# Modulation weights in 64 pieces of 32 rows by quarter columns, with the sum over partitions on VectorE instead of TensorE

## The reference

```
c_act = silu(c)
for i in range(2):
    mod = c_act @ w_ada[i] + b_ada[i]              # w_ada[i]: 1024 x 6144
    sh_a, sc_a, g_a, sh_f, sc_f, g_f = split(mod, 6)
    h = rmsnorm(x) * (1 + sc_a) + sh_a
    m = neighbourhood_attention(h) if i == 0 else mla(h)
    x = x + g_a * m
    h = rmsnorm(x) * (1 + sc_f) + sh_f
    f = swiglu(h) if i == 0 else moe(h)            # moe: 8 experts, top 2
    x = x + g_f * f
return rmsnorm(x) * final_norm
```

## Time and profile before

| | us |
|---|---|
| three runs | 1257.86, 1258.61, 1263.98 |
| median of the three | 1258.61 |
| profiled execution: span from the first to the last instruction | 1258.0 |
| mean granted TensorE clock, as a share | 0.996 |

### The profile page before, as it was taken

How to read it: one execution, slowest core, us unless ns; L and a number is a source line. 1 busy time by engine, 2 the same in 40 slices (tenths; PEclk the granted TensorE clock), 3 DMA queues, 4 the chain that set the end, 5 groups by cost and what they waited for, 6 DMA issues and landing times.

```text
span 1258.0 us, 20244 instructions
## 1 busy us (share of the span) xinstructions
PE 1224.1 (97%) x7668; PEld 1086.8 (86%) x7668; DVE 1016.2 (81%) x1095; ACT 779.0 (62%) x992; POOL 93.1 (7%) x111
## 2 busy tenths in 40 slices
PE   9989999999999999999999999999999999999995
PEld 7978999987998799998897777898989898989884
DVE  6797899996756588777756578989898989898987
ACT  5765666644655455443346556777777777777764
POOL 0020000000562100000002202000000000000020
PEclk9999999999999999999999999999999999999998
DMA  9953997679944569998973239999999999999991
GB/s 322 377 200 102 337 314 270 246 289 252 250 159 162 181 215 325 332 349 308 382 253 97 79 140 394 379 406 355 401 351 409 348 408 349 408 345 411 347 410 73
DMA packets 163981, 369.08 MB, mean 293 GB/s; under 512 B 24420, under 2 KB 96559, under 8 KB 157511
## 3 DMA queue, kind: packets, MB, share of 16 engines
q1 hardware_dynamic: 157345, 350.72, 78.0%
q10 hardware_dynamic: 5094, 12.11, 2.5%
q0 software_dynamic: 1472, 5.28, 1.1%
HBM read 360.72 MB, written 14.70 MB: 298 GB/s over the span
## 4 chain that ended last, share of the span: by engine, by line
PE 71%; DVE 12%; ACT 4%; issue 4%; DMA 3%; SPq 3%; POOL 2%; ACTq 0%; DVEq 0%
PE ps L1341 20%; PE ps L795 7%; PE ps L797 7%; PE ps L796 7%; PE ps L1368 6%; PE ps L807 4%; PE ps L809 4%; PE ps L811 4%; DVE wlo L1893 3%; SPq L712 2%; PE ps L859 2%; PE ps L867 2%; DMA raw<-in_moe_w_gu 2%; DVE third_lo L1893 2%; DVE wlo L1885 1%
## 5 line engine op out<-in xcount | busy, mean ns | idle before, releaser
L1406 ACT ACTIVATE whi<-raw 128x1024 fp32r<-128x1024 f32 x186 | 192.6, 1057 | 152.0 <-PE ps L797 96.1
L1885 DVE TENSOR_TENSOR wlo<-raw,whi 128x1024 fp32r<-128x1024 f32 x186 | 227.1, 1248 | 72.8 <-ACT whi L1406 69.3
L795 PE MATMUL ps<-ahi,whi 128*128 128x256 f32 x832 | 234.3, 282 | 0.3 <-ACT qT L1591 0.3
L796 PE MATMUL ps<-alo,whi 128*128 128x256 f32 x832 | 231.8, 279 | 0.0
L797 PE MATMUL ps<-ahi,wlo 128*128 128x256 f32 x832 | 231.8, 279 | 0.0
L1893 DVE TENSOR_TENSOR wlo<-raw,whi 128x1792 fp32r<-128x1792 f32 (+1 forms) x96 | 199.3, 2089 | 24.4 <-ACT whi L1420 24.3
L1420 ACT ACTIVATE whi<-raw 128x1792 fp32r<-128x1792 f32 (+1 forms) x96 | 167.5, 1758 | 55.9 <-PE ps L1368 24.0
L795 PEld LDWEIGHTS ps<-ahi,whi 128*128 128x128 f32 x832 | 156.9, 189 | 1.7 <-issue 0.8
L796 PEld LDWEIGHTS ps<-alo,whi 128*128 128x128 f32 x832 | 156.7, 188 | 0.7 <-issue 0.7
L797 PEld LDWEIGHTS ps<-ahi,wlo 128*128 128x128 f32 x832 | 156.9, 189 | 0.0
L1341 PE MATMUL ps<-whi,hchi 128*128 128x448 f32 x352 | 101.8, 370 | 4.0 <-DVE wlo L1893 2.7
(11 more groups left out here) (350 smaller groups left out, 2431.7 us busy)
## 6 DMA issues: line engine op xcount, KB each, us to landing
raw<-in_moe_w_gu SPq DMA_DIRECT2D x96, 896.0 KB, 7.0
ada<-in_w_ada SPq DMA_DIRECT2D x48, 1024.0 KB, 7.4
raw<-in_moe_w_down SPq DMA_DIRECT2D x32, 1024.0 KB, 7.9
ada<-in_moe_w_gu SPq DMA_DIRECT2D x32, 896.0 KB, 7.3
raw<-in_w_up SPq DMA_DIRECT2D x22, 1024.0 KB, 5.8
raw<-in_ffn_w_gu SPq DMA_DIRECT2D x22, 1024.0 KB, 9.1
ada<-in_moe_w_down SPq DMA_DIRECT2D x16, 1024.0 KB, 9.2
raw<-in_na_w_qkv SPq DMA_DIRECT2D x12, 1024.0 KB, 8.4
```

The lines of the kernel that those rows point to most:

```text
L795: pe.matmul(o, h[:, k, cols], bhi[:, k], start=(k == 0), stop=False)
L796: pe.matmul(o, h[:, k, cols], blo[:, k], start=False, stop=False)
L1406: act.activation(high_, src, ACT.Copy).then_inc(hi_done, 1)
L1885: ve.tensor_tensor(low_, src, high_.bitcast(F32), ALU.subtract).then_inc(lo_done, 1)
```

## The change

w_ada is laid out anew on the host: a piece is 32 rows by 6144 columns, set as 128 partitions of 1536 columns (a group of 32 partitions holds 32 rows of a quarter of the columns), contiguous, 768 KB with runs of 6 KB. There are 32 of them in a layer and one accumulator `acc`, 128x1536; c is repeated four times over partitions to match. The columns are ordered so that, after a transposition of 32x32 blocks and a sum over groups of 32, `mod` has 6 x 8 columns: shifts and scales with feature k*128 + p on partition p, gates with feature p*8 + k. `modulation(layer)` on VectorE, after DOWN and after DOWN2, does that in a transpose, a reduction, an addition of the biases and one of 1 to the scales. TensorE sums nothing any more. GpSimd sends the gates to memory (`send_gates`) and loads each back as a row broadcast to all partitions (`spread_gates`); VectorE waits for these rows in `residual_gate`. ScalarE's loads of the biases, VectorE's `shifts` and `gate_rows`, and their semaphores go. The vectors are laid out as columns on the host and come in two loads; the transposes and the copies go. The pieces are placed anew: 8 in IN (steps 1 to 6, two in steps 2 and 4), 2 in OUT, 1 in norm1, 12 in UP (in the steps 1 to 10, two in 5 and 10), 9 in DOWN for layer 0; 2 in NAO, 1 after norm3, 18 in GU, 11 in DOWN2 for layer 1. The two slots stay, and so does the union of buffers, 1 KB further up. The rotary table's load now stands behind layer 1's `spread_gates`.

```
+IN_PIECES = {1: [0], 2: [1, 2], 3: [3], 4: [4, 5], 5: [6], 6: [7]}
...
+ADA_MIX, ADA_UP, ADA_DOWN = zip(_plan_pieces(ADA_IN, 3, [0, 1, 1, 1, 1, 2, 1, 1, 1, 1, 2], [1, 1, 2, 1, 1, 2, 1]),
+                                _plan_pieces(0, 3, [1, 2, 2, 1, 2, 2, 1, 2, 2, 1, 2], [2, 1, 2, 1, 2, 1, 2]))
...
-                part, k = j // KT, j % KT
-                src = a["w_ada_2"][layer][k * P:(k + 1) * P, part * ADA_COLS:(part + 1) * ADA_COLS]
-                sp.dma_start(ada[:, g % NADA], src).then_inc(ada_in[g % NADA], 16)
+                sp.dma_start(ada[:, g % NADA, 0:ADA_COLS], a["w_ada_2"][layer, j]).then_inc(ada_in[g % NADA], 16)
...
-            load_rows(["b_conv_ffn"], "rows_in")
+            sp.dma_start(vecs[:, 0:VEC_EARLY], a["vecs"][:, 0:VEC_EARLY]).then_inc(sem("vecs_in"), 16)
...
                     sp.wait_ge(mm_done, 2 * W_QKV)
+                    sp.wait_ge(sem("mods_ready"), 1)
                     for n in range(GR):
                         load_bias2(1, n)
...
-            sum_columns(0, (0,), 3)
-            whole_columns(W_UP, 1, (0, 1), lambda: sum_columns(0, (1,), 3, KT))
-            pe.wait_ge(sem("mod_read0"), 1)
+            whole_columns(W_UP, 1, (0, 1))
...
-                part, k = j // KT, j % KT
-                o = acc[layer][part]
-                ck = vec("c")[:, k:k + 1]
+                src, ck = ada[:, g % NADA, 0:ADA_COLS], vec("c")[:, j:j + 1]
                 ve.wait_ge(ada_in[g % NADA], 16 * (g // NADA + 1))
...
+            def modulation(layer):
+
+                ve.wait_ge(ada_used, NADA + ADA_CHUNKS * (layer + 1))
+                own.link(ve.transpose(acc_turned, acc))
+                own.link(ve.tensor_reduce(mod, acc_turned.rearrange("p (n r) -> p n r", r=ADA_ROWS), AXX, ALU.add))
                 b = vec("b_ada")[:, layer * 6 * KT:(layer + 1) * 6 * KT]
...
+                own.link(ve.tensor_tensor(mod, mod, b, ALU.add))
+                scales = mod.rearrange("p (h m k) -> p h m k", h=2, m=3)[:, :, 1]
+                own.link(ve.tensor_scalar(scales, scales, 1.0, None, ALU.add))
+                ve.sem_inc(sem("mods_ready"), 1)
...
                     if t == 0:
+                        ve.wait_ge(sem("gates_in"), 32 * ((s - 2) // 2 + 1))
                         ve.wait_ge(sem("tile_done"), s + 1)
...
-            down(W_DN2, DN_CHUNKS, 1, range(ADA_DOWN[1], ADA_CHUNKS))
-            shifts(1, (0, 1, 3), 0, 2)
-            norm_by_tile(4, sc_a, sh_a, residual_gate(3, W_MDN), None, lambda: shifts(1, (4,), 3, 3))
...
+            down(W_DN2, DN_CHUNKS, 1, ADA_DOWN[1])
+            modulation(1)
+            norm_by_tile(4, sc_a, sh_a, residual_gate(3, W_MDN))
...
+            def send_gates(layer):
+
+                po.wait_ge(sem("mods_ready"), layer + 1)
+                src = mod.rearrange("p (h m k) -> p h m k", h=2, m=3)[:, :, 2]
+                po.dma_start(gate_dram[layer].rearrange("g (p k) -> p g k", k=KT), src).then_inc(sem("gates_out"), 16)
+
+            def spread_gates(layer):
+
+                po.wait_ge(sem("gates_out"), 16 * (layer + 1))
+                for g in range(2):
+                    po.dma_start(gate_row[layer][g], gate_dram[layer, g:g + 1].broadcast_to([P, D])).then_inc(sem("gates_in"), 16)
+
             attention(1, range(H1))
+            send_gates(0)
             mask_bias2(0)
+            spread_gates(0)
             attention(2, range(4))
             mask_bias2(1)
             attention(2, range(4, H2))
+            send_gates(1)
+            spread_gates(1)
             po.wait_ge(mm_done, 2 * W_MDN)
             po.dma_start(rope, a["consts"][:, C_ALL:C_ALL + R_ALL]).then_inc(sem("rope_in"), 16)
             attention(3, range(H2))
-            po.wait_ge(sem("gate_read1"), 4)
+            po.wait_ge(sem("x_ready"), NT * 4)
```

More of the change, by code:

```diff
@@ L100, with _plan_pieces, take @@
 W_MOE = W_MLO + 4
[L102 to L111, removed]
+ADA_ROWS = 32
+ADA_CHUNKS = D // ADA_ROWS
+ADA_COLS = 6 * D // (P // ADA_ROWS)
+IN_PIECES = {1: [0], 2: [1, 2], 3: [3], 4: [4, 5], 5: [6], 6: [7]}
+ADA_IN = 8
+def _plan_pieces(first, mix, steps, chunks):
+    n = [first]
+    def take(count):
+        n[0] += count
+        return list(range(n[0] - count, n[0]))
+    plan = take(mix), [take(c) for c in steps], [take(c) for c in chunks]
+    assert n[0] == ADA_CHUNKS
+    return plan
+ADA_MIX, ADA_UP, ADA_DOWN = zip(_plan_pieces(ADA_IN, 3, [0, 1, 1, 1, 1, 2, 1, 1, 1, 1, 2], [1, 1, 2, 1, 1, 2, 1]),
+                                _plan_pieces(0, 3, [1, 2, 2, 1, 2, 2, 1, 2, 2, 1, 2], [2, 1, 2, 1, 2, 1, 2]))
 VEC = {}
 def _plan_vectors():
[L118 to L124, removed]
-    at = 0
[L126 to L137, removed]
+    at = 0
+    for name, count in (("c", ADA_CHUNKS), ("g_pre_mix", 8), ("g_pre_ffn", 8), ("w_conv_lru", 16), ("b_conv_lru", 4),
+                        ("b_r", 4), ("b_i", 4), ("lam", 4), ("q_norm", 2), ("kv_norm", 1), ("b_conv_ffn", 44),
+                        ("b_ada", 96), ("w_conv_ffn01", 88), ("w_conv_ffn2", 44)):
+        VEC[name] = (count, at)
+        at += count
+    return VEC["b_ada"][1], at
+VEC_EARLY, VEC_COLS = _plan_vectors()
 C_ID, C_IOTA, C_TRI, C_ONE = 0, 128, 256, 384
@@ L661, in load_ffn @@
                     load(gu + c)
-                for n in ADA_UP[layer].get(0, []):
+                for n in ADA_UP[layer][0]:
                     load_ada(layer, n)
@@ L665, in load_ffn @@
                     load(gu + NRAW + 2 * j)
-                    for n in ADA_UP[layer].get(j + 1, []):
+                    for n in ADA_UP[layer][j + 1] if j + 1 < GU_STEPS else []:
                         load_ada(layer, n)
@@ L669, in load_ffn @@
                 c = 2 * GU_STEPS + NRAW
-                for j in range(ADA_DOWN[layer], ADA_CHUNKS):
-                    load_ada(layer, j)
+                for pieces in ADA_DOWN[layer]:
+                    for j in pieces:
+                        load_ada(layer, j)
                     if layer or gu + c < W_QKV - 1:
@@ L919, in output_chunk, with output_projection @@
                     done(m)
-            def output_projection(first, k_all, bhi, blo, s, gated=None, after=None, begun=0, last=None, inside=None):
+            def output_projection(first, k_all, bhi, blo, s, gated=None, begun=0, last=None, inside=None):
                 chunks = k_all // 2
@@ L1474, in ld @@
                 act.dma_start(dst, src).then_inc(sem(s), n)
-            for name, (tile, row, count, _) in VEC.items():
-                if name not in SP_ROWS:
-                    ld(rows[row:row + count, tile, :], VEC_SRC[name](a), "rows_in")
             def exponentials(n, i, slot, src, scale, bias):
@@ L1916, in modulate_tile, with norm_by_tile @@
                         modulated(hx[:, t, k], src, k, scale, shift).then_inc(mods_done["dve"], 1)
-            def norm_by_tile(s, scale, shift, residual=None, piece=None, between=None):
+            def norm_by_tile(s, scale, shift, residual=None, piece=None):
                 if piece:
@@ L2241, in gate_up_conv @@
                         product(j - 1, 1)
[L2242 removed]
+                    for n in ADA_UP[0][j]:
                         modulate_part(0, n)
```

229 lines of the change are left out of this document (65 added, 164 removed).

## The result

The changed kernel is slower by 0.6%: 1268.68 us in the median of ten runs (1264.65 to 1272.85), the kernel before 1262.48 in the median of ten (1257.6 to 1264.7), ratio 1.0057 with the 95% interval 1.0041 to 1.0073. Forecast were 1249.8 us and a ratio of about 0.993.

A forecast was written before the change was run, and what follows sets the result against it. It took TensorE (busy 1224 of 1258.0 us) as the bound, corrected by the chain of waits through SP's loads and GpSimd in QKV. Its terms summed to -8.8, a span of 1249.2, measured as 1249.8 us; range 1242 to 1263.

The forecast's parts named there:

- step 5: Vectors as columns, fewer loads and no copies: 0; among the first heads, eight pieces of 1.8 for six of 2.35: 0.
- step 2 (c): DOWN2: eleven smaller pieces through two slots come each 2.8 to 3.5 us, just enough; +1.0 us, bounds 0 and +4.
- 2.0 + 1.7: DOWN: nine pieces through two slots delay the last use, +2.0; two pieces ahead of the split between UP and DOWN, +1.7.
- the 4 that the prediction gave: Sign of being right: first small load of the attention tables up to 4 us later, counted from the end of UP.
- my 0.75 of the old landing: Lower end for a smaller piece's landing, 0.75 x 7.4 = 5.6 us over the run; 3.8 in DOWN2, from 5.1.
- 5.4 + 0.9: Sums off TensorE in DOWN2: 3.57 + 1.78 give -5.4; the block at 632.36, taken by half, gives -0.9.
- (C): Rival: delivery through two slots, past its turning point, makes the kernel slower; landing 8.5 gives +8.5, 1267.1 us; chance 0.12.
- one of the signs of being right: Pieces that land in 5.6 to 6.7 us over the run.
- The rotary table: Layer 1: its load is queued behind the gates' send and spreading on GpSimd; +1.0 us, bounds 0 and +4.
- MLA: Four head steps with a gate, GpSimd's idle time falling from 3.03 to 2.55 us in each: -1.9 us.
- (D): Rival: VectorE's transpose runs at the reciprocal's pace, 12.8 us in all with its sum; +7.6, 1266.2 us; chance 0.05.
- (A): Rival: all 23.6 us of sums taken off TensorE count, as it is 97% busy; 1235 us; chance 0.07.

The follow-up runs named there:

- the rotary load ahead: Changed kernel with layer 1's rotary table load issued on GpSimd after the gates are sent but ahead of the loads that spread them; ratio 1.0054 to the kernel before.
- both: Changed kernel with three slots of 1536 columns and the rotary table's load issued ahead of the spreading of the gates; ratio 0.9947 to the kernel before.
- the new places: Layer 0 pieces moved against the changed kernel: IN six, one a step, UP 13, DOWN 10; rotary table loaded before gate spreading; 0.9896 with three slots, 1.0019 with two.
- without pieces: Changed kernel with only each layer's first piece loaded and accumulated, 62 of 64 left out; read only to the MoE's first matmul, no whole-time ratio given.
- the pair: Changed kernel without 62 of 64 pieces, and kernel before with 6 of 48 pieces; marks at the MoE's first matmul 10.6 us apart.

## Why the prediction was wrong

**The step that failed is the delivery of the pieces: the 0 of step 5 for those in IN, and the +1.0 of step 2 (c) for DOWN2.** For DOWN the prediction went by the round of a slot, half of landing plus use for each piece. There 2.0 + 1.7 were forecast and 3.7 measured. A third slot takes 2.1 us off DOWN between two runs in which the clock did not fall there (64.07 with the rotary load ahead, 61.95 with three slots), near the 2.0. Where it fell it takes only 0.7 (64.24 in the changed kernel, 63.58 with both), so that the sum came out to a tenth is in part luck. The first small load of the attention tables, counted from the end of UP, came 5.3 us later (49.3 after it, for 44.0 before), over the 4 that the prediction gave. For IN step 5 said "eight of 1.8 stand for six of 2.35: 0", a sum of VectorE's busy time alone. The row to read was the landing in IN, from 18 to 64 us, in the kernel before:

```profile
ada<-in_w_ada SPq DMA_DIRECT2D x6, 1024.0 KB, 9.7
```

By it six rounds of (9.7 + 2.35)/2 are 36 us. Eight of 1.8 are 36 to 46, for a landing between three quarters of 9.7 and all of it: between 0 and 10 us more, where 0 was put. In the changed kernel it was

```profile
ada<-in_w_ada SPq DMA_DIRECT2D x8, 768.0 KB, 9.1
```

A piece each (9.1 + 1.8)/2 = 5.5 us is 44 us for eight, from 18.66 to 62.5 in the chain. The round describes IN but does not bound it, since a third slot moved no piece there: the bound is the 364 GB/s that the DMA engines move, without a pause, before and after. The bytes of the pieces in IN stayed as they were (8 x 768 KB for 6 x 1024), and the pairs in steps 2 and 4 ask for them sooner. With the new places and two slots the first turn of norm1 comes at 118.75 instead of 124.98, 117.05 before. So what was put at 0 is the larger part of the +8.8 of this stage; the wait ahead of norm1 and the clock behind it are the rest.

**DOWN2 was mis-sized.** I took 2.8 to 3.5 us a piece from a landing of 3.8 to 5.1. The pieces land in 5.5 there in the median, later than the larger ones of before (5.1); two are now asked for one behind the other, between weights, which may be why. In the chain it is 5.4 to 8.3. So my 0.75 of the old landing does not hold in this stage: it is 1.08, and 0.78 over the run. Here the slots are the bound: DOWN2 takes 59.87 us with three of them and 59.87 without pieces, 67.03 before and 67.25 in the changed kernel. So the sums gave 7.2 us there, for 5.4 + 0.9 (the last block came off whole and not by half), and the delivery that was put at +1.0 took 7.4 (5.5 to 6.3 in four other runs with two slots). The Trainium skill's fixed part (DMA: Bandwidth & Descriptors, Anatomy of one DMA — SWDGE (gpsimd) path) had, by an estimate, 0.86 of the old landing, and the trace does not agree in this stage either.

**Of the rivals it was (C)**, in its mechanism and its sign, but not at the point that it named: pieces land in 5.8 us in the median, not over 7.5, and by its formula 17 refills at 5.8 take 64.6 of the 67.3 us that they had, no delay at all. That its price, 1267.1, is near the measured 1268.68 is luck: it put 20.3 us into DOWN and DOWN2, where some 2 and 7 were found, and IN and the rotary table, which its sum did not have, made up for part of that. The landing of 5.8 us was also one of the signs of being right, and told nothing. Stalls cost more than their length, since the clock fell behind some of them. The prediction named such a fall at its end as something that would break the sum, and gave it no price.

**The rotary table** was +1.0 with bounds to +4, and +3.1 to +3.8 were found. What was not sized is the wait for the send's landing: 256 runs of 32 bytes took 10.7 us, and GpSimd waits for it in its order. The table's own landing was 3.0 us longer as well, and with the spreading behind it 0.3.

**Right** were the sums: without pieces the pair is 10.6 apart with the 3.8 of the rotary table in it, against 14.5 less that. So were MLA (GpSimd's idle time of a step is 2.55, as forecast, from 3.03 in the earlier trace rows), the turn of the accumulator and the absence of (D):

```profile
697.85 1.84 POOL L2496 TENSOR_SCALAR probs<-probs,small 128x256 f32<-128x256 f32 x4 [2.55 <-DVE small L1924]
```

The Trainium skill's one element per cycle and lane for a transpose (Vector Engine (DVE) Microarchitecture Reference, 3.8 The reshape front-end and per-opcode configuration) was an estimate of 1.6 us; 1.77 were measured, so the trace agrees within 0.2 us. (A) fell with the QKV stage, 4.3 us shorter and not 10.

**Open** is the size of the clock's share in the whole. The profiles differ by 13 us where the medians differ by 6.2: the changed kernel's is the slowest of its ten, and 4.3 us of it are GU's pace. The spans of the ten runs tend to go with the mean granted clock (1262.8 us at 0.989, 1271.0 at 0.985), which fits stalls after which the clock falls in some executions and not in others; no run took that apart. Open is also what sets the pace of GU, and how many of the runs had which.

## What to carry to other kernels

Size a stream through a few slots by its round, landing plus use over the number of slots, in every stage that it passes, with the landing of that stage and not of the run. More and smaller pieces can need more slots, even if bytes and busy time stay, as in DOWN2. Where the DMA engines already have no time to spare, as in IN, another slot only makes the landing longer, and what helps is to ask for less, or later: a plan that asks for two pieces in a step asks for bytes sooner. Read a stall of TensorE as longer than it may look, compare profiles stage by stage before a difference is put down to a change, and compare kernels whose values steer the work only up to the point where they do.

## What the runs showed of the hardware

After a stall of 4.16 us TensorE's pairs followed each other in 0.85 us for 0.455, and a stall of 5.59 us cost another 1.5 by the clock, which filling it with matmuls gave back. The clock did not fall at every stall, and not by length: it fell at stalls of 1.76 and 1.83 us and stayed full after the 2.64 us for the rotary table, all in the changed kernel. Ahead of norm1 two runs show the same stall of 3.16 us and the same work behind it, with three slots: without the new places the clock was at 0.50 from 124 to 126 us, with them it stayed full.

TensorE can be busy all the time at a full clock and still go at two paces. In GU, with the same code, it did 797 matmuls in 90 us in some profiles and 767 in others, 120.40 and 124.66 us for the stage.

A third slot in a stage where the DMA engines are busy all the time (shares of 1.07 and 1.08 from 18 to 60 us) moved no piece, and the landing of a piece grew from 9.1 to 11.5 us.

A small DMA can be slow: a send of 8 KB in 256 runs of 32 bytes, issued while weights filled the queues (a DMA share of 1.12 from 638 to 650 us), took 10.7 us to land, as long as the chain waited for a weight load of 1 MB in the earlier trace rows (10.26). The same send took 5.4 us in layer 0, at a share of 1.11 from 310 to 322 us, so the share alone does not give it.
